# A two-layer transformer kernel: GpSimd takes a share of two tile-turning stages and of the beginning of layer 1's sums

## The reference

```
for l in range(DEPTH):
    sh_a, sc_a, g_a, sh_m, sc_m, g_m = modulation(c, w_mod[l], b_mod[l])   # one row per condition
    h = x * (1 + sc_a) + sh_a
    y = mixer_ab(h, ...) if l == 0 else mixer_c(h, ...)
    x = layer_norm(ALPHA * x + g_a * y, ln1_g[l], ln1_b[l])
    h = x * (1 + sc_m) + sh_m
    x = layer_norm(ALPHA * x + g_m * (relu(h @ w1[l]) ** 2 @ w2[l]), ln2_g[l], ln2_b[l])
```

## Time and profile before

| | |
|---|---|
| time of three runs | median 2968.99 us (2968.83 to 2974.59) |
| the profiled execution | 2971.22 us, its span 2969.4 us |
| TensorE (PE) | 2793.5 us busy, 94% |
| VectorE (DVE) | 1367.4 us, 46% |
| ScalarE (ACT) | 887.6 us, 30% |
| GpSimd (POOL) | 533.5 us, 18% |
| mean granted clock | 0.973 |

### The profile page before, as it was taken

How to read it: one execution, slowest core, us unless ns; L and a number is a source line. 1 busy time by engine, 2 the same in 40 slices (tenths; PEclk the granted TensorE clock), 3 DMA queues, 4 the chain that set the end, 5 groups by cost and what they waited for, 6 DMA issues and landing times. The chain is left out here.

```text
span 2969.4 us, 40552 instructions
## 1 busy us (share of the span) xinstructions
PE 2793.5 (94%) x15615; PEld 2289.2 (77%) x15615; DVE 1367.4 (46%) x2195; ACT 887.6 (30%) x1598; POOL 533.5 (18%) x365
## 2 busy tenths in 40 slices
PE   6999996999999999999969999999697999999998
PEld 3666785788888888888858888888585888888886
DVE  3575554663333333333573565555556333333336
ACT  3244653441211211211132443444342211221222
POOL 0000000341121121111320000000133323323321
PEclk8999998999999999999989999999898999999999
DMA  7584216440010110110331111100455111111112
GB/s 260 189 309 149 75 63 225 123 133 29 29 56 28 39 46 28 42 42 28 85 114 50 36 44 37 36 29 15 129 141 149 57 42 42 57 42 42 57 42 57
DMA packets 202132, 237.42 MB, mean 80 GB/s; under 512 B 15960, under 2 KB 165088, under 8 KB 195872
## 3 DMA queue, kind: packets, MB, share of 16 engines
q1 hardware_dynamic: 201728, 235.74, 24.9%
q10 hardware_dynamic: 288, 0.10, 0.0%
HBM read 203.20 MB, written 36.83 MB: 81 GB/s over the span
## 5 line engine op out<-in xcount | busy, mean ns | idle before, releaser
L2106 DVE TENSOR_TENSOR y<-y,pair 128x1024 f32<-128x1024 f32 x280 | 341.7, 1221 | 337.4 <-PE pair L2275 337.4
L2273 PE MATMUL pair<-m_wbh,m_ath 128*128 128x512 f32 x1080 | 422.1, 391 | 16.8 <-DVE y L2041 16.8
L2275 PE MATMUL pair<-m_wbh,m_atl 128*128 128x512 f32 x1080 | 423.2, 392 | 0.0
L2274 PE MATMUL pair<-m_wbl,m_ath 128*128 128x512 f32 x1080 | 422.2, 391 | 0.0
L1947 ACT ACTIVATE m_rel<-pair 128x512 f32<-128x512 f32 x160 | 88.9, 556 | 1021.0 <-PE pair L2297 1009.9
L2163 DVE TENSOR_TENSOR m_atl<-m_sq,m_ath 128x512 fp32r<-128x512 f32 x150 | 96.4, 644 | 623.1 <-POOL m_sq L2000 623.1
L2000 POOL TENSOR_TENSOR m_sq<-m_rel 128x512 f32<-128x512 f32 x160 | 155.5, 972 | 1124.7 <-ACT m_rel L1947 1124.5
L2297 PE MATMUL pair<-hth,m0n_wal 128*128 128x512 f32 (+1 forms) x768 | 272.2, 354 | 0.0
L2296 PE MATMUL pair<-htl,m0n_wah 128*128 128x512 f32 (+1 forms) x768 | 272.1, 354 | 0.0
L2295 PE MATMUL pair<-hth,m0n_wah 128*128 128x512 f32 (+1 forms) x768 | 271.6, 354 | 0.0
L2273 PEld LDWEIGHTS pair<-m_wbh,m_ath 128*128 128x128 f32 x1080 | 203.4, 188 | 60.7 <-issue 16.3
(11 more groups left out here) (284 smaller groups left out, 5283.7 us busy)
## 6 DMA issues: line engine op xcount, KB each, us to landing
a_ring<-in_w_mod SPq DMA_DIRECT2D x40, 1024.0 KB, 9.4
m_rawb<-in_mlp_w SPq DMA_DIRECT2D x64, 512.0 KB, 4.4
m_rawa<-in_mlp_w SPq DMA_DIRECT2D x60, 512.0 KB, 4.1
x_rows<-r_res SPq DMA_DIRECT2D x26, 512.0 KB, 5.4
r_raw<-cat_cols SPq DMA_DIRECT2D x18, 512.0 KB, 6.4
mod_w<-in_w_mod SPq DMA_DIRECT2D x8, 1024.0 KB, 12.2
r_xin<-in_x SPq DMA_DIRECT2D x16, 512.0 KB, 12.4
gate_pre<-a0g_gout SPq DMA_DIRECT2D x20, 256.0 KB, 2.0
```

Source lines behind the costliest of these rows:

```text
L2106: dve.tensor_tensor(k.y[:, t, :], k.y[:, t, :], k.pair[t % 2][:, :], ALU.add).then_inc(s_y, 1)
L2273: pe.matmul(o, ath[:, m, ts], bh[:, m, cols], start=m == 0, stop=False)
L2274: pe.matmul(o, ath[:, m, ts], bl[:, m, cols], start=False, stop=False)
L2275: i = pe.matmul(o, atl[:, m, ts], bh[:, m, cols], start=False, stop=m == M - 1)
```

## The change

In both tile-turning stages the subtraction of every fourth step goes from VectorE to GpSimd, with a semaphore `s_pl` of its own; ScalarE waits for whichever engine has the low half of four steps before.

In `stage_block`, SyncE loads the gate of the frames and the first residual ahead of `lng` and `lnb`, and the other gate (layer 0) last. The gates have semaphores of their own (`s_rg`), for which VectorE waits; it no longer waits for the rows.

In layer 1, GpSimd multiplies the loaded x by `ln1[0]` (`weigh`), and VectorE, which has scaled `ln1[1]` by ALPHA once, does y = ALPHA * y + that in one instruction for each tile. GpSimd's `weigh` of tiles 0 to 2 stands ahead of its multiplication of w2's first chunk by the gate, the others between its squares of chunk 0. VectorE's tiles 1 to 4 stand behind the low halves of group 0, and 5 to 7 behind those of group 1.

```diff
@@ stage_first; stage_between alike, with placed(...) and in_rows(...) @@
+    by_pool = lambda i: i % 4 == 3
+    lows = [sum(not by_pool(x) for x in range(i)) for i in range(len(steps) + 1)]
+    s_pl = sem("pl")
...
         def _(pool):
             k.clear_last(pool)
+            for i, (a, n, kt) in enumerate(steps):
+                if by_pool(i):
+                    hi, v = k.hth[:, kt, a:a + n], modt[:, i % NB, 0:n]
+                    pool.wait_ge(s_ha, i // 2 + 1)
+                    pool.tensor_tensor(k.htl[:, kt, a:a + n], v, f32(hi), ALU.subtract).then_inc(s_pl, 1)
...
-                if i >= NB:
-                    act.wait_ge(s_hl, i - NB + 1)
+                if i >= NB and by_pool(i - NB):
+                    act.wait_ge(s_pl, i // NB)
+                elif i >= NB:
+                    act.wait_ge(s_hl, lows[i - NB + 1])
...
-                dve.tensor_tensor(k.htl[:, kt, a:a + n], v, f32(hi), ALU.subtract).then_inc(s_hl, 1)
+                if not by_pool(i):
+                    dve.tensor_tensor(k.htl[:, kt, a:a + n], v, f32(hi), ALU.subtract).then_inc(s_hl, 1)
@@ stage_block, SyncE @@
+            def gate_in(c):
+                sp.dma_start(rgate[:, c, :].rearrange("p (j q) -> p j q", q=P),
+                             bass.AP(tensor=k.gate_dram.tensor, offset=(layer * 2 * 2 * KT + c) * P, ap=[[0, P], [2 * P, KT], [1, P]])).then_inc(s_rg[c], 16)
+
+            gate_in(0)
+            residual_in(0)
             for t, name in ((lng, "ln2_g"), (lnb, "ln2_b")) if final else ((lng, "ln1_g"), (lnb, "ln1_b")):
                 sp.dma_start(t[:, :], bass.AP(tensor=io[name].tensor, offset=0, ap=[[0, P], [1, D]])).then_inc(s_row, 16)
-            for c in range(3 - XB):
-                sp.dma_start(rgate[:, c, :].rearrange("p (j q) -> p j q", q=P),
-                             bass.AP(tensor=k.gate_dram.tensor, offset=(layer * 2 * 2 * KT + c) * P, ap=[[0, P], [2 * P, KT], [1, P]])).then_inc(s_row, 16)
-            for t in range(XB):
+            for t in range(1, XB):
                 residual_in(t)
+            for c in range(1, 3 - XB):
+                gate_in(c)
@@ stage_block, GpSimd @@
-            pool.wait_ge(s_row, 48 if final else 64)
+            pool.wait_ge(s_row, 32)
...
+            def weigh(t):
+                if t == 0:
+                    pool.wait_ge(s_begin, 32)
+                pool.wait_ge(s_yx[t], 16)
+                y = by_j(k.y[:, t, :])
+                pool.tensor_tensor(y, y, ln1[0], ALU.mult).then_inc(s_past, 1)
+
             def step(c):
...
+                if starts(c) and final:
+                    for t in range(3):
+                        weigh(t)
...
                         pool.tensor_tensor(sq[:, m % 2, 0:n], r, r, ALU.mult).then_inc(s_sq, 1)
+                        if starts(c) and final:
+                            for t in ((), (3, 4), (5,), (6, 7))[g * M + m]:
+                                weigh(t)
@@ stage_block, VectorE @@
                     if final:
-                        dve.wait_ge(s_yx[t], 16)
                         y = by_j(k.y[:, t, :])
                         if t == 0:
                             dve.wait_ge(s_begin, 32)
-                        dve.scalar_tensor_tensor(out=y, in0=y, scalar=ALPHA, in1=ln1[0], op0=ALU.mult, op1=ALU.mult).then_inc(s_past, 1)
+                            dve.tensor_scalar(ln1[1], ln1[1], ALPHA, None, ALU.mult).then_inc(s_shift, 1)
+                            dve.wait_ge(s_shift, 1)
                         dve.wait_ge(s_past, 2 * tiles + t + 1)
-                        dve.scalar_tensor_tensor(out=y, in0=ln1[1], scalar=ALPHA, in1=y, op0=ALU.mult, op1=ALU.add).then_inc(s_y, 1)
+                        dve.scalar_tensor_tensor(out=y, in0=y, scalar=ALPHA, in1=ln1[1], op0=ALU.mult, op1=ALU.add).then_inc(s_y, 1)
...
-            dve.wait_ge(s_row, 48 if final else 64)
...
+                dve.wait_ge(s_rg[cond(t)], 16)
                 dve.wait_ge(s_yps, t + 1)
...
-                        if final and starts(c):
-                            begin_y(1, tiles)
                     for m in range(M):
...
+                    if final and starts(c):
+                        begin_y(*((1, 5), (5, tiles))[g])
```

More of the change, by code:

```diff
@@ L279, in _ @@
                 hi, v = k.hth[:, kt, a:a + n], modt[:, i % NB, 0:n]
-                dve.wait_ge(s_mod, i + 1)
-                if by_act(i):
+                if by_pool(i):
+                    pass
+                elif by_act(i):
+                    dve.wait_ge(s_mod, i + 1)
                     dve.wait_ge(s_ha, i // 2 + 1)
                 else:
+                    dve.wait_ge(s_mod, i + 1)
                     dve.tensor_copy(hi, v).then_inc(s_hd, 1)
                     dve.wait_ge(s_hd, i // 2 + 1)
-                dve.tensor_tensor(k.htl[:, kt, a:a + n], v, f32(hi), ALU.subtract).then_inc(s_hl, 1)
+                if not by_pool(i):
+                    dve.tensor_tensor(k.htl[:, kt, a:a + n], v, f32(hi), ALU.subtract).then_inc(s_hl, 1)
         @block.tensor
@@ L1176, in _ @@
             k.clear_last(pool)
+            for i, (a, n, kt) in enumerate(steps):
+                if by_pool(i):
+                    hi, v = placed(k.hth, kt, a, n), in_rows(modt[:, i % NB, :], a, n)
+                    pool.wait_ge(s_ha, i // 2 + 1)
+                    pool.tensor_tensor(placed(k.htl, kt, a, n), v, f32(hi), ALU.subtract).then_inc(s_pl, 1)
         @block.scalar
@@ L1215, in _ @@
                 hi, v = placed(k.hth, kt, a, n), in_rows(modt[:, i % NB, :], a, n)
-                dve.wait_ge(s_mod, i + 1)
-                if by_act(i):
+                if by_pool(i):
+                    pass
+                elif by_act(i):
+                    dve.wait_ge(s_mod, i + 1)
                     dve.wait_ge(s_ha, i // 2 + 1)
                 else:
+                    dve.wait_ge(s_mod, i + 1)
                     dve.tensor_copy(hi, v).then_inc(s_hd, 1)
                     dve.wait_ge(s_hd, i // 2 + 1)
-                dve.tensor_tensor(placed(k.htl, kt, a, n), v, f32(hi), ALU.subtract).then_inc(s_hl, 1)
+                if not by_pool(i):
+                    dve.tensor_tensor(placed(k.htl, kt, a, n), v, f32(hi), ALU.subtract).then_inc(s_hl, 1)
                 if i in later:
@@ L1685, in stage_block @@
     rsem = lambda n: k.sem(f"{rtag}_{n}")
-    s_row, s_xr, s_past, s_begin = rsem("rows"), [rsem(f"x{i}") for i in range(XB)], rsem("past"), rsem("begin")
+    s_row, s_xr, s_past, s_begin, s_shift = rsem("rows"), [rsem(f"x{i}") for i in range(XB)], rsem("past"), rsem("begin"), rsem("shift")
     s_raw = [rsem(f"raw{i}") for i in range(2)]
@@ L1689, in stage_block @@
     s_dve, s_std, s_g, s_b, s_tr, s_mod, s_hh, s_hl, s_half = [rsem(x) for x in ("dve", "std", "g", "b", "tr", "mod", "hh", "hl", "half")]
+    s_rg = [rsem(f"rgate{c}") for c in range(2)]
     s_lnr, s_lnt, s_fold = rsem("lnr"), rsem("lnt"), rsem("fold")
```

1 line of the change is left out of this document (added).

## The result

| | median (all runs) |
|---|---|
| kernel before | 2970.58 us (2968.83 to 2974.59, 7 runs) |
| kernel after | 2982.07 us (2979.27 to 2983.64, 7 runs) |
| ratio | 1.0039, 95% interval 1.0030 to 1.0049 |

The kernel after takes 11.5 us more (8.9 to 14.6 by the interval). The forecast was 2980.0 us, +11.0. The profiled execution of after took 2979.27 us, its span is 2977.5 us; it is the fastest of the seven. Against the span before, 2969.4, the two profiles show only 8.1 us.

The account below looks back on a forecast made before the run. TensorE, busy 94% of the span, was taken as the bound, so only its idle stretches count. Terms +14.7 - 6.7 + 0 + 0.5 + 2.5 = +11.0 on the median of 2968.99 gave 2980.0 us, range 2968 to 2988.

Parts of the forecast that it names:

- How the engines share: VectorE and GpSimd take turns by whole instructions: VectorE's 1024-wide ones take about 3.3 us beside GpSimd, 1.22 alone.
- Layer 1's beginnings, +14.7: Layer 1: tile 6 ready at 2289, TensorE's restart +15.7, less 0.96 for the eighth tile; bounds +3.6 and +17.
- the stretches stay as many: Layer 1: half-speed stretches of TensorE behind idle time stay two, as before.
- The rival of the floor: Layer 1: GpSimd's next-chunk work is held up, tile 6 at 2278 to 2283, +3.7 to +8.7, 2969 to 2974; chance 0.2.
- Parallel after all: Layer 1: GpSimd's pieces don't hold up VectorE, tile 6 ready at 2268, kernel faster at 2956; chance 0.12.
- Layer 0's residual, -6.7: Layer 0: early gate and first residual gain 6.9 us, perhaps 0.2 goes back; bounds -7 and -3.
- no wait is left: Layer 0: first residual row ready at 518.2, TensorE arrives at 518.6, so its 4.65 us wait goes.
- Layer 1's residual, 0: Layer 1: the same four loads precede GpSimd's first instruction, so TensorE's 11.0 us wait stays; -0.5 to +0.5.
- The turning stages, +0.5 and +2.5: Tile-turning stages: first +0.5 (0 to +2) from GpSimd's last low half; second +2.5 (-0.6 to +5), delaying VectorE's normalisation.
- the rival of slow short runs: Tile-turning stages: GpSimd is slow on short runs, both stages cost 8 together, total 2985; chance 0.1.
- +2 for the second stage if casts don't wait: Second turning stage: cost is +2 instead of +2.5 if VectorE's casts don't wait beside GpSimd.
- The sum: Whole kernel: +14.7 - 6.7 + 0 + 0.5 + 2.5 = +11.0, giving 2980.0 us.

Follow-up runs that it names:

- e4: Kernel after plus one wait: in layer 1 GpSimd starts chunk 1's low halves only when all eight sums are begun; 2973.23 us.
- e7: Kernel before plus one wait: GpSimd does not split chunk 1's first weights until all eight beginnings are done; 2964.07 us.
- e1: Kernel before with only the edit of layer 1's beginnings (GpSimd's share of them); 2984.10 us.
- e9: e5 with one load moved: layer 0's third-tile columns issued right after the first residual; 2956.72 us.
- e2: Kernel before with only the new order of gate and residual loads and their separate semaphores; 2966.43 us.
- e3: Kernel before with only the edit of the two tile-turning stages; 2973.91 us.
- e8: Kernel before with the turning-stage edit, but in the second stage GpSimd takes its fourth steps only from step 8 on; 2970.50 us.
- e5: Kernel before with the new gate/residual load order, GpSimd held until all eight beginnings are done, and VectorE beginning tiles 0 to 2 early, keeping both products; 2957.24 us.

## Why the prediction was right, step by step

**How the engines share: right.** From 2237.7 to 2282.3 both timelines of layer 1 alternate, except in one idle stretch of VectorE, at the prices of the earlier trace rows: 3.3 to 3.4 us for VectorE's 1024-wide instructions beside one of GpSimd's of that width, and 2.3 to 3.4 for GpSimd's. e4 and e7 moved only GpSimd's instructions and VectorE's went back to 1.2 us.

**Layer 1's beginnings, +14.7: right in mechanism, and nearly in size.** The start was forecast as tile 0's sum ended at 2246.6, the split at 2249.9, the wait for y near 26 us. The last tile's transposes came 5.76 us earlier in after, so these are 2240.8 and 2244.1 there; measured were 2240.98 and 2244.26, and the wait was 25.8. The restart moved by 16.0 instead of 15.7. The end of the kernel moved by less than the restart, by 13.9: D is 2.2 shorter, of which 0.96 was forecast (the wait for the eighth tile) and the rest was not. Behind the restart only 8 matmuls were slow where before it had been 12, at 0.2 us each another 0.8; the forecast had said the stretches stay as many, and took them as equally long. e1 alone gives +13.3.

**The rival of the floor: wrong, for the reason given.** GpSimd was not held up by a load, and brought its next chunk's work forward by turns. e4 shows what the floor is worth: with that work taken away the kernel lands at 2973.2, inside the 2969 to 2974 of that rival. **Parallel after all** is excluded by e1 and by the 3.3 us and more of five of the eight sums.

**Layer 0's residual, -6.7: right in mechanism, too large.** No wait is left and the first transposes take 1.03 us, as was listed. VectorE did not even wait for its gate (the earlier trace rows has 9.36 us for it; in after the row names TensorE as what ended the wait), and the first row was ready at 516.05, when TensorE came for it at 518.21. VectorE in after, 509 to 524:

```profile
509.98 0.17 DVE L2102 COPY r_lnc<-pair 128x16 f32<-128x16 f32 x1 [5.17 <-PE pair L2308]
...
515.24 0.81 DVE L2143 TENSOR_SCALAR r_res<-r_res,r_mv,r_rstd 128x1024 f32<-128x1024 f32 x1
```

The step that failed is "no wait is left", read as if nothing else could be late: the term of -6.7 was mis-sized and measures -4.4 to -4.5. A projection that begins at half speed paid nothing before, because the wait took it up, and pays now: 4.65 + 2.3 - 2.4 = 4.55 us in after. And the third tile's split, put down at 0.2, costs 1.3 where the projection begins with more full-speed matmuls, by the later load and by a turn of GpSimd, which the forecast had priced for layer 1 and not looked for here. Both kinds of start give the same A, between 133.8 and 134.2 in five kernels and e9; without the edit A is 138.3 to 138.6 where the start was at full speed and 139.1 and 139.7 where it was not.

**Layer 1's residual, 0: right.** TensorE's longest wait there is 11.2 us against 11.0; it lay between 11.0 and 11.7 in the five kernels without the new order and between 9.5 and 11.6 in the six with it.

**The turning stages, +0.5 and +2.5: right in mechanism, too large by some 0.9.** The 512-wide subtraction takes 1.26 to 1.29 us beside little else (estimate 1.28), and the first two with short runs in the second stage 1.29 and 1.35 (two later ones, which start while VectorE's normalisation or subtraction runs, 1.85 and 1.66), so the rival of slow short runs is wrong. B grew by 2.6, but 0.8 of this is the first transposes, which took 5.99 us in after and 5.20 in before; e2, which has no edit there, shows 5.99 and a B longer by 0.8 too. In e3 and e4, where they took 5.04 and 5.26, B is 1.7 and 1.9 longer.

ScalarE's own distances give both stages more sharply. From its first modulation to its last high half the first stage takes 21.5 us in all eleven profiles, so the edit costs nothing up to there; from that last high half to the next stage's first matmul it takes 1.15 us with the edit and 0.85 without, because the last low half, 256 wide, is GpSimd's:

```profile
56.24 0.72 POOL L266 TENSOR_TENSOR htl<-r_modt,hth 128x256 fp32r<-128x256 f32 x1 [1.98 <-ACT hth L273]
```

That is +0.3 where +0.5 was forecast. In the second stage the first distance is 24.15 us without the edit, 25.7 with it and 24.27 in e8; the second grows by 0.3 as well. So it costs 1.8, of which 1.4 comes from the two subtractions ahead of the last normalisation. The forecast had charged these as two whole GpSimd instructions less one subtraction saved, 1.9. But the two VectorE instructions began when GpSimd's were already under way and were lengthened by only 0.94 and 1.06, which less 0.69 is 1.3. Behind them it had 0.6 and got 0.4.

The Trainium skill ("SBUF — State Buffer", section "Who interferes with whom") says that copies and casts contend too in a 2-port mode. In the first turning stage of after a cast that started beside GpSimd took twice its time:

```profile
39.45 0.93 DVE L297 CAST hth<-r_modt 128x512 fp32r<-128x512 f32 x1 [0.84 <-ACT r_modt L282]
...
41.63 0.42 DVE L297 CAST hth<-r_modt 128x512 fp32r<-128x512 f32 x1
```

The trace agrees with the page here (0.93 and, in the second stage, 1.48 against 0.42). The forecast had +2 for the second stage if casts don't wait; they do, and it came out at 1.8 for the reason just given.

**The sum.** By medians the parts are +13.3, -4.4 and +3.1 against +14.7, -6.7 and +3.0 as forecast. By the distances in the trace of after they are +13.9 (C and D), -4.5 (A) and +0.3 and +1.8, together +11.5. The terms of layer 1 and of the turning stages were too large, and so was layer 0's gain, with the opposite sign; that +11.0 came so near to +11.5 is in part luck, because they cancel. Of the 2.1 us between 2980.0 and 2982.07 the other 1.6 is the kernel before, 2968.99 in three runs and 2970.58 in seven.

## What to carry to other kernels

Ask of work that is moved from VectorE to GpSimd what each of the two costs on the way that they share: here 2.3 us for what VectorE does in 1.2, so the move lengthened both. Before that, look at what GpSimd has queued behind the needed work: in these traces they take turns while both have something to do, however little hurry one of them is in, and a single wait that held two of its splits back, and the products behind them, was worth 6.5 us by the medians (3.6 to 9.5). Where a wait is removed, ask what it had been hiding.

## What the runs showed of the hardware that was not expected

- The clock at the start of a stage differs between executions of nearly the same program. Layer 0's projection began at full speed in before, e3 and e7, ran five matmuls at full speed and then eight at half in e4 and e5, and began at half speed in the six others. The ten matmuls of `keep_busy` ahead of it ran at half speed, 0.43 us each, in all eleven, but for the last three of e8. In the projection all six kernels with the new order of loads had a slow stretch, and two of the five without it; the loads are issued only some 9 us after the projection begins, so no way is seen by which they could cause it, and it is left open whether this is chance. It is worth up to 2.5 us.
- The length of the half-speed stretch behind a long idle time isn't fixed either: behind the restart of layer 1 it was between 7 and 13 matmuls in the eleven profiles, 13 in e5 and 7 in e9 behind the same 12.5 us of waiting. At 0.43 us for a matmul against 0.23 that is up to 1.2 us of the 3.9 by which D varies.
- Unchanged stages of 430 us differ by up to 4 us from one execution to another, more than most terms of this case. The difference of two whole profiles (8.1 us) missed the 11.5 of the medians; distances between instructions inside a stage did not.
